# GpSimd's row gathers ahead of the low-half subtraction, in one inference step of a hybrid encoder with PEER

## The reference, cut to what matters

```
p  = x @ w_in                              # q, k, v of two attentions, two gates
h  = LN1(alpha*x + (sigmoid(gA)*(yA@w_proj_a) + sigmoid(gB)*(yB@w_proj_b)) @ w_out)
q  = h @ w_query                           # 8 heads, two halves of 128
e, gate = product_key_top16(q, sub_keys)   # 16 of 128*128 experts per head
act = gelu(sum_d u[e] * h)                 # one row of u_table per token and pick
y  = LN2(alpha*h + sum_picks gate*act * v[e])
```

## Time and profile before

| | us |
|---|---|
| median of 3 runs (4509.64 to 4519.65) | 4511.42 |
| the profiled execution | 4520.74 |
| its span, first to last instruction | 4519.0 |
| TensorE busy | 4078.8 (90%) |
| VectorE busy | 2960.8 (66%) |
| GpSimd busy | 2972.8 (66%) |
| ScalarE busy | 1614.2 (36%) |
| mean rate of all DMA | 296 GB/s |

### The profile page before, as it was taken

One profiled execution on the slowest core, in us unless ns is written; L12 is line 12 of the kernel. 1 busy time (PEld: TensorE's weight loads), 2 busy tenths in 40 slices (PEclk: granted clock), 3 DMA queues, 4 the chain that ended last, 5 costly groups with the idle time before them and its releaser, 6 DMA issues. The chain is left out here.

```text
span 4519.0 us, 71127 instructions
## 1 busy us (share of the span) xinstructions
PE 4078.8 (90%) x26453; PEld 3895.8 (86%) x26453; DVE 2960.8 (66%) x4328; ACT 1614.2 (36%) x2677; POOL 2972.8 (66%) x1624
## 2 busy tenths in 40 slices
PE   7989999999979999997999999888998998977867
PEld 7978889999967887896999999888898997867867
DVE  3034542277557898966967977677677777768665
ACT  3433334443223334323334863232322232322223
POOL 6844447675744555773567568788888887867764
PEclk9989889999989999998999999999999999989888
DMA  8655447554967787993459899999999999989983
GB/s 257 207 170 167 124 119 209 166 167 144 392 270 305 299 348 300 383 351 116 124 172 367 294 322 413 385 418 416 416 407 418 418 418 388 414 347 368 382 329 120
DMA packets 361554, 1336.27 MB, mean 296 GB/s; under 512 B 35456, under 2 KB 143872, under 8 KB 275840
## 3 DMA queue, kind: packets, MB, share of 16 engines
q0 software_dynamic: 93760, 682.66, 37.1%
q1 hardware_dynamic: 141696, 510.20, 33.0%
q10 hardware_dynamic: 125888, 140.75, 9.0%
HBM read 1275.11 MB, written 63.18 MB: 296 GB/s over the span
## 5 line engine op out<-in xcount | busy, mean ns | idle before, releaser
L466 POOL TENSOR_TENSOR w_lo<-w_raw,w_hi 128x1024 fp32r<-128x1024 f32 x968 | 2342.6, 2421 | 1147.9 <-ACT w_hi L928 1121.2
L928 ACT ACTIVATE w_hi<-w_raw 128x1024 fp32r<-128x1024 f32 x968 | 1019.4, 1056 | 1266.3 <-DMA w_raw<-in_wstream 522.3
L1423 DVE CUSTOM_DVE_ANT_0 rows<-rows,banks 128x2048 f32<-128x2048 f32 x320 | 730.6, 2283 | 251.6 <-DMA rows<-in_u_rows,idx_all 249.9
L865 PE MATMUL banks<-weighted,w_hi 128*128 128x320 f32 x3328 | 768.9, 321 | 135.5 <-DVE weighted L1800 63.0
L1426 DVE SCALAR_TENSOR_TENSOR banks<-rows,act_n,banks 128x2048 f32<-128x2048 f32 x320 | 752.2, 2351 | 194.9 <-DMA rows<-in_v_rows,idx_all 191.7
L531 PE MATMUL banks<-mv,w_hi 128*128 128x256 f32 x3648 | 697.8, 293 | 35.1 <-POOL w_lo L466 28.8
L809 PE MATMUL banks<-mv_hi,w_hi 128*128 128x320 f32 x2048 | 657.4, 321 | 61.8 <-POOL w_lo L466 57.2
L865 PEld LDWEIGHTS banks<-weighted,w_hi 128*128 128x128 f32 x3328 | 582.3, 197 | 146.0 <-DVE weighted L1800 66.9
L531 PE MATMUL banks<-mv_hi,w_hi 128*128 128x384 f32 x1824 | 635.6, 348 | 36.8 <-ACTq L1194 21.5
L809 PE MATMUL banks<-mv_lo,w_hi 128*128 128x320 f32 x2048 | 642.0, 313 | 0.0
L809 PE MATMUL banks<-mv_hi,w_lo 128*128 128x320 f32 x2048 | 641.7, 313 | 0.0
(11 more groups left out here) (175 smaller groups left out, 5279.7 us busy)
## 6 DMA issues: line engine op xcount, KB each, us to landing
w_raw<-in_wstream SPq DMA_DIRECT2D x968, 512.0 KB, 4.4
gate_matrix<-work ACTq DMA_DIRECT2D x20, 1024.0 KB, 10.6
work<-gate_matrix ACTq DMA_DIRECT2D x16, 1280.0 KB, 10.2
early_act<-work ACTq DMA_DIRECT2D x48, 160.0 KB, 5.7
work<-early_act ACTq DMA_DIRECT2D x48, 160.0 KB, 23.2
out_p<-work ACTq DMA_DIRECT2D x34, 192.0 KB, 3.5
gate_scratch<-work ACTq DMA_DIRECT2D x32, 192.0 KB, 7.4
work<-gate_scratch ACTq DMA_DIRECT2D x16, 384.0 KB, 8.4
```

The source lines that it names most:

```text
L466: pool.tensor_tensor(w_lo[s][:, part], raw[s][:, part], w_hi[s][:, part].bitcast(f32), ALU.subtract) \
L865: last = pe.matmul(banks[:, dt % 4, 0:ND], a[s][:, at:at + P], b[z][:, e, :], start=(e == 0 and n == 0), stop=(e == EG - 1 and n == 2))
L928: act.activation(w_hi[s][:, HALVES[h]], raw[s][:, HALVES[h]], ACT.Copy).then_inc(hi_late, 1)
L1423: ins = dve.tensor_tensor_reduce(rows, rows, nat, 1.0, 0.0, ALU.mult, ALU.add, weight)
```

## The change

GpSimd's loop issues the gathers of a part first and subtracts behind them. Nothing else is different: the same instructions, the same waits with them, the same steps.

```diff
             for n in range(GATHER_AT, TOTAL):
                 first = (len(STEPS[n]) + 1) // 2
                 for h, part in enumerate((STEPS[n][:first], STEPS[n][first:])):
-                    if n + 2 < TOTAL:
-                        low(n + 2, n % 2, h)
                     for r in part:
                         if ITEMS[r][0] == "c":
                             rows = rows_t[place(r)]
                             pool.wait_ge(half_copied, 1)
                             pool.dma_start(rows[0:G3, :], rows[G3:P, :]).then_inc(rows_in[place(r)], 16)
                         if ITEMS[r][0] == "b":
                             norm_store(r, ITEMS[r][1])
                         if r + ROWS < len(ITEMS):
                             fetch(r + ROWS)
+                    if n + 2 < TOTAL:
+                        low(n + 2, n % 2, h)
```

## The result

The changed kernel takes 4598.81 us (median of 4 runs, 4593.86 to 4600.82); the kernel before, on the same chip, 4513.12 us. The ratio is 1.0176, 95% interval 1.0158 to 1.0194. The forecast was 4510 us and no change: wrong, by 89 us. The medians are 85.7 us apart, the spans of the two profiled executions (4599.0 and 4519.0) 80.0; what follows accounts for the 80.

The account below looks back on a forecast made before the run. The prediction took full DMA engines, shared by gathered rows and weights, as the bound. Its terms 2 + 0 + 0 - 1.3 + 0 - 2.3 = -1.6 us gave 4510 us, own range 4500 to 4519, 8-in-10 range 4492 to 4534.

Parts of the forecast that it names:

- Second attention to query units: Second attention through query units: gathers leave up to 2.4 us earlier, but rows are early there, so 0.
- a slot of 3.6 us: GpSimd's queue: one gather, subtraction and gap, 3.6 us, by which low weight halves come later; a single loss allowed in range.
- C: Slower rival: the lag reaches VectorE at 11 u-to-v steps of the regular stage, +52 us, 4563 us; chance 0.06.
- First gather stage: Units 136 to 147: unit 147 and its store 3.6 us late, between 0 and +3.6 passed on; taken as +2.
- Early units: Early units from 2376 us on: lag absorbed at full DMA engines, 0; one slot of 3.6 us lost is in range.
- Regular stage: Regular stage, 160 units: TensorE's later start absorbed by its waits, 0; half a unit of weights not fetched ahead, -1.3.
- B: Faster rival: gathers bound by their own latency, so earlier ones land earlier; -27 us more, 4483 us; chance 0.17.
- Last groups: Last groups: stored activations issued 3.6 us later in 3 groups, landing unmoved at full DMA engines; 0, ends 0 and +10.8.
- A: Slower rival: late issue passed on in the last groups and first gather stage, +12 us, 4523 us; chance 0.21.
- The copy rows<-rows: Copy joining the last block's halves: issued ahead of a 2.34 us subtraction instead of behind it, -2.3, ends 0 and -3.5.
- the DMA line: Profile page's busy tenths: DMA said to stand at 9 from 2600 us on until the last two slices.

Follow-up runs that it names:

- all_but_att: Gathers ahead of the subtraction everywhere except in the 32 steps of the second attention, where the kernel before's order stays: 4513.2 us, ratio to before 0.9994.
- att_only: Gathers ahead of the subtraction only in the 32 steps of the second attention, the kernel before's order everywhere else: 4602.99 us, ratio to before 1.0193.
- wait_only: Kernel before, order kept, but in the second attention the subtraction first waits until VectorE has released the row of its part: 4550.27 us, ratio 1.0072.
- behind_scale: Changed kernel, but in the second attention the subtraction behind the gather also waits for VectorE's next softmax scaling to be done: 4511.63 us, ratio to before 0.9997.

## Why the prediction was wrong, point by point

**The step that failed** is "Second attention to query units: the gathers come ahead of a subtraction, up to 2.4 us earlier, but rows are early there ... 0. The cover is its own work". It asked only whether the moved gathers matter to VectorE, and they didn't. It never asked what the moved *subtraction* does to VectorE: measured +77.1 us, and +5.2 in the projections and queries behind it. Two readings were missing. The waits of GpSimd, 1280 to 1741, had `w_lo` behind ScalarE for 226.7 us in 47 waits, so this was no queue that "runs back to back or waits for VectorE"; the swap would change who releases the subtraction. And the line L1544 already had instructions of up to 2.47 us beside a median of 0.35 in the kernel before, not in this stage but in the first attention: ten of the 64 scalings there took 1.86 to 2.47 us, each beside a subtraction, where the others took 0.29 to 0.36. That was the price, on show. 90 scalings held for a whole subtraction of 2.4 us each, 216 us, would have been a rough upper bound of this term; the prediction had none there but a slot of 3.6 us.

**The rivals** all dealt with lags and gathers; none had this mechanism. The slower one nearest in time, C, asked for losses at the u-to-v steps of the regular stage, where nothing was lost.

**The rest held**, as all_but_att shows by itself: 0.9994, that is -2.7 us (-7.7 to +2.3) where the sum said -1.6. Term by term:

- First gather stage, +2 between 0 and 3.6: unit 147 is late by 3.0 to 3.8 us as worked out (b4 99.9 to 102.9 and 103.7), but nothing of it is passed on: b4 and attention together take 602.9 to 604.9 us in the four kernels with the new order in b4, whole subtractions and no long scalings in the attention, against 606.3 before. The end "0" of the bound was the right one.
- Early units, 0 with a slot of 3.6 in the range: the slot is lost, +3.0 to +3.8 in the new-order kernels with single subtractions.
- Regular stage, 0 and -1.3: 1344.2 to 1349.4 us with the new order, 1343.9 to 1346.4 with the old. TensorE's waits moved as forecast, from weighted to `w_lo`, though by more than the "some us": after,

```profile
PE banks L809 <- POOL w_lo L466: 58.1, 18, 16.2
PE banks L865 <- POOL w_lo L466: 48.2, 10, 20.4
PE banks L865 <- DVE weighted L1800: 24.7, 10, 7.5
```

  against 56.9 + 11.0 (the second is of line 865) and 59.1 before, and the stage lost nothing by it; that goes against C. VectorE's waits for rows stayed, 187.7 and 147.6 us against 187.2 and 146.2, and the rate with them (404 GB/s); that refutes B.
- Last groups, 0: the loads of early_act leave 1.2 us later after the regular stage's end in the first group and land 3.5 us sooner, in 25.63 us instead of 30.38, and VectorE's waits for them are the same. A late issue wasn't passed on, and A is refuted; but the landing came earlier, where the prediction had it stay:

```profile
DVE work L1796 <- DMA work<-early_act: 79.1, 5, 16.7
```

- The copy rows<-rows, -2.3 (0 to -3.5): VectorE now waits 0.65 us for it instead of 5.61. The last part takes 499.4 to 503.8 us in the kernels of the new order and 504.4 to 508.1 in those of the old, some 5 us less on average, so the term had the right sign and was too small, if it is this copy alone; no run separates it.

```profile
4502.03 2.29 DVE L1442 TENSOR_TENSOR banks<-banks,rows 64x2048 f32<-64x2048 f32 x1 [0.65 <-DMA rows<-rows]
```

Of the size of the loss one piece stays unplaced: the 5 us behind the attention (proj_b to query_b 495.3) appear with held scalings (after, att_only, wait_only 493.1) and go with them, by a path that no view here follows; and how much the lower granted clock adds to the 77 us stays open. One reading of the prediction was loose without harm: the DMA line isn't at 9 all the way from 2600 us, one slice (3955 to 4068 us) reads 8.

## What to carry to other kernels

Before two instructions of a queue are swapped, look up for each, in every stage, what releases it now and what would release it then: an instruction newly released by another engine's step comes at a nearly fixed point of that engine's cycle. Then list what it runs beside at that point, and look in the trace of before for the same pair already overlapping: a group whose longest instruction is seven times its median has the price in it. If the meeting can't be avoided, a form of the instruction that doesn't share the port (0.61 us for 2.92; the whole 4513.75 us) is cheaper than cutting the other engine's work in pieces (4549.73), and so is a wait that puts the other engine's instruction behind it (4511.63).

## What the runs showed of the hardware

- A subtraction of GpSimd with two inputs in SBUF holds up a plain `tensor_scalar` of VectorE in SBUF until 0.08 to 0.30 us behind its own end: 57 such cases in the changed kernel's trace, up to 3.33 us for one of 512 columns (0.49 alone) and 3.01 for one of 256 (0.35). By these ends it isn't a slowdown but a stop.
- Who is first can't be read from these two starts alone: in 47 of the 57 the scaling's record begins 0.18 to 0.63 us *before* the subtraction's, and it is held all the same. In all 47 a gather of GpSimd is running at that moment, ends 0.15 to 0.61 us later, and the subtraction stands 0.02 us behind it. Where no gather ran, a lead of 0.12 us was enough (8 cases of 256 columns, not held). How the gather takes part no run isolates; alone it costs a scaling 0.17 us at most (behind_scale).
- Comparisons on VectorE with two SBUF inputs (L1784) are held too, 2.88 us instead of 0.68. Not held beside the same subtraction: the row steps, which read PSUM for one input (L1423 and L1426, 2.28 and 2.35 us with and without), and the copy from PSUM (L1551).
- The accumulating form costs 0.13 us more at 256 columns (479 against 353 ns) and 0.26 us at 512 (746 against 486), with 83 ns for reading the accumulator. Four pieces of 256 columns keep GpSimd busy for 2.94 us against 2.42 for 1024 at once, so (2.94 - 2.42) / 3 = 0.17 us for each further instruction.
